# A hybrid DiT step with product-key experts: key numbers summed on Pool, and another passage from gates to experts

## What is computed

```python
def peer(h, wq, keys, u, v):
    q = (x @ wq).reshape(t, PEER_HEADS, 2, PEER_HALF)
    sc = jnp.einsum('thpc,hpnc->thpn', q, keys)
    s_top, i_top = lax.top_k(sc, PEER_TOPK)
    cand = (s_top[:, :, 0, :, None] + s_top[:, :, 1, None, :]).reshape(t, PEER_HEADS, -1)
    cs, ci = lax.top_k(cand, PEER_TOPK)
    i1 = jnp.take_along_axis(i_top[:, :, 0], ci // PEER_TOPK, axis=-1)
    i2 = jnp.take_along_axis(i_top[:, :, 1], ci % PEER_TOPK, axis=-1)
    idx = i1 * PEER_N_KEYS + i2
    g = jax.nn.softmax(cs, axis=-1)
    a = jnp.einsum('thkd,td->thk', u[idx], x)
    act = jax.nn.gelu(a, approximate=False) * g
    return jnp.einsum('thk,thkd->td', act, v[idx])
```

## Time and profile before

| | |
|---|---|
| three runs | 3451.32, 3452.62, 3455.44 us; median 3452.62 |
| the profiled execution | 3446.14 us, its span 3444.0 us |
| busy in the span | PE 91%, DVE 85%, Pool 54%, ACT 31% |
| mean granted PE clock | 0.958 |
| layer 0: routing, gates, experts | 461 to 655, 655 to 784, 784 to 1867 |
| layer 1: routing, gates, experts | 1980 to 2198, 2198 to 2327, 2327 to 3410 |

### The profile page before, as it was taken

How to read it: one execution, slowest core, us unless ns; L and a number is a source line. 1 busy time by engine, 2 the same in 40 slices (tenths; PEclk the granted TensorE clock), 3 DMA queues, 4 the chain that set the end, 5 groups by cost and what they waited for, 6 DMA issues and landing times.

```text
span 3444.0 us, 50075 instructions
## 1 busy us (share of the span) xinstructions
PE 3141.0 (91%) x15686; PEld 2593.3 (75%) x15686; DVE 2929.7 (85%) x5454; ACT 1053.0 (31%) x1587; POOL 1860.0 (54%) x1415
## 2 busy tenths in 40 slices
PE   7898999398999999999998795398999999999997
PEld 4455555277999999999997463377899999999996
DVE  2654189897999999999998599887999999999998
ACT  2132111143333333333333210243333333333332
POOL 0000023485677877776673033585777777766663
PEclk9999999699999999999999897699999999999999
DMA  4131253148999999999996010149999999999995
GB/s 203 49 122 53 92 213 135 49 213 349 408 410 409 402 403 383 410 407 410 398 407 256 25 49 0 73 195 376 397 410 409 408 402 396 406 409 400 408 401 206
DMA packets 244489, 994.43 MB, mean 289 GB/s; under 512 B 22592, under 2 KB 72512, under 8 KB 204864
## 3 DMA queue, kind: packets, MB, share of 16 engines
q0 software_dynamic: 147456, 536.94, 39.5%
q1 hardware_dynamic: 96960, 456.52, 33.3%
HBM read 940.15 MB, written 53.22 MB: 288 GB/s over the span
## 4 chain that ended last, share of the span: by engine, by line
PE 78%; DVE 13%; issue 4%; DMA 3%; POOL 1%; ACT 1%; DVEq 0%; POOLq 0%; SPq 0%; ACTq 0%
PE bankA L1143 10%; PE bankA L1145 10%; PE bankA L1144 10%; PE bankD L1131 6%; PE bankD L1156 6%; PE bankD L1157 6%; PE bankD L1155 6%; PE bankA L1235 5%; PE bankA L1157 3%; PE bankA L1156 3%; PE bankA L1155 3%; PE bankD L1281 2%; DMA rows<-in_u,idxc 2%; PE bankA L1227 1%; DVE topi L873 1%
## 5 line engine op out<-in xcount | busy, mean ns | idle before, releaser
L514 POOL DMA_INDIRECT rows<-in_u,idxc x512 | 736.8, 1439 | 238.1 <-issue 132.8
L514 POOL DMA_INDIRECT rows<-in_v,idxc x512 | 661.1, 1291 | 267.5 <-issue 128.2
L1143 PE MATMUL bankA<-hh,uh 128*128 128x384 f32 x2048 | 690.0, 337 | 23.6 <-ACT htok L584 13.8
L1145 PE MATMUL bankA<-hh,ul 128*128 128x384 f32 x2048 | 689.6, 337 | 0.0
L1144 PE MATMUL bankA<-hl,uh 128*128 128x384 f32 x2048 | 688.2, 336 | 0.0
L1005 DVE SCALAR_TENSOR_TENSOR acc<-rows,a,acc 128x1024 f32<-128x1024 f32 x512 | 634.3, 1278 | 6.7 <-DMA rows<-in_v,idxc 5.5
L996 DVE CUSTOM_DVE_ANT_0 rows<-rows,htok 128x1024 f32<-128x1024 f32 x512 | 607.2, 1218 | 25.3 <-DMA rows<-in_u,idxc 22.8
L476 POOL TENSOR_TENSOR mask<-mask,topf 128x1280 f32<-128x1280 f32 x32 | 91.8, 2891 | 818.7 <-DVE mask L924 818.7
L568 ACT ACTIVATE wt<-bankA 128x384 f32<-128x384 f32 x256 | 125.9, 492 | 1064.8 <-PE bankA L1145 848.7
L1143 PEld LDWEIGHTS bankA<-hh,uh 128*128 128x128 f32 x2048 | 386.4, 189 | 36.3 <-ACT htok L584 14.4
L1156 PE MATMUL bankD<-vl,wh 128*128 128x512 f32 x1024 | 399.8, 390 | 0.0
(11 more groups left out here) (181 smaller groups left out, 4484.0 us busy)
## 6 DMA issues: line engine op xcount, KB each, us to landing
uraw<-in_uT SPq DMA_DIRECT2D x128, 1024.0 KB
vraw<-in_vP SPq DMA_DIRECT2D x128, 1024.0 KB
gates_scratch<-gbuf SPq DMA_DIRECT2D x12, 4096.0 KB, 11.6
gp<-gates_scratch SPq DMA_DIRECT2D x64, 768.0 KB
sq<-in_ada SPq DMA_DIRECT2D x14, 2048.0 KB, 7.9
wch<-in_ada SPq DMA_DIRECT2D x10, 2048.0 KB, 7.9
wch<-in_wq SPq DMA_DIRECT2D x8, 2048.0 KB, 8.0
rows<-in_u,idxc POOLq DMA_INDIRECT x512
```

The costliest lines, as they stand in the source:

```text
L514: pool.indirect_dma_start(out=rows[:, j, :], out_offset=None, in_=table.rearrange("l e d -> (l e) d"), in_offset=bass.IndirectOffsetOnAxis ...
L1143: pe.matmul(abank[c], hi, hh[:, k, :], start=k == 0, stop=False)
L1145: last = pe.matmul(abank[c], lo, hh[:, k, :], start=False, stop=k == K - 1)
```

## The change

- Pool makes the key numbers alone (`pick_keys`): one fold of both masks from 16 columns to 8, then to 4, to 2, and two adds that write i12. DVE's `key_numbers` is gone; DVE waits for mask_scaled before it writes topf, and for mask_done before it writes mask. All eight heads' i12 are waited for by mask_done after the softmax.
- hl is computed by Pool, between heads 6 and 7. hh is cast by ACT as soon as the scores are copied, before the Exp, and the transposes to htok come before the gates.
- Each gate stage of Pool is followed by three gathers (the third by two). The first five row buffers lie in hT, which nobody reads any more by then.
- The last block of gates is stored in two parts: key numbers 0 to 7 first (256 KB), then, behind the load of v pair 1, the rest (3840 KB). dense_begun comes when the last gate is copied, without waiting for a store; v pair 0 is loaded at once, gates 0 to 3 after the small store, gates 4 to 7 after the rest has landed. acc is cleared between the rows of u and those of v.
- Buffers lie elsewhere in SBUF.

```diff
         with ExitStack() as dn:
-            hh = sb("hh", [P, K, TD], F32R, where=dn)
-            hl = sb("hl", [P, K, TD], F32R, where=dn)
+            htok = sb("htok", [P, GT, D], where=dn)
             uraw = sb("uraw", [P, 2, 2 * D], where=dn)
+            rowsB = sb("rowsB", [P, RING - TILES, D], where=dn)
             uh = sb("uh", [P, 2, D], F32R, where=dn)
             ul = sb("ul", [P, 2, D], F32R, where=dn)
             vraw = sb("vraw", [P, 2, 2 * D], where=dn)
...
+            gp1 = sb("gp1", [P, TD // TB, 4, TB], where=dn)
+            acc = sb("acc", [P, GT, D], where=dn)
+            gap = sb("gap", [P, 5440], where=dn)
+            hh = sb("hh", [P, K, TD], F32R, where=dn)
+            hl = sb("hl", [P, K, TD], F32R, where=dn)
             wl = sb("wl", [P, 2, TD], F32R, where=dn)
-            gp = sb("gp", [P, 2, TD // TB, 4, TB], where=dn)
-            rows = sb("rows", [P, RING, D], where=dn)
-            htok = sb("htok", [P, GT, D], where=dn)
-            acc = sb("acc", [P, GT, D], where=dn)
+        gp = (gp0, gp1)
+        hrows = hT[:, :, :].rearrange("p k t -> p (k t)").rearrange("p (r d) -> p r d", d=D)
+        row_buf = [hrows[:, j, :] if j < TILES else rowsB[:, j - TILES, :] for j in range(RING)]
+        htok_bank = [bankA[0], bankD[1]]
...
@@ -362,7 +370,15 @@
                 for b in range(TD // TB):
                     n = L * (TD // TB) + b
                     sp.wait_ge(g_out, (n + 1) * (TB // HOT) + 2)
-                    sp.dma_start(gates_d[b], gbuf[:, b % 2, :, :]).then_inc(stored[b % 2], 16)
+                    if b < TD // TB - 1:
+                        sp.dma_start(gates_d[b], gbuf[:, b % 2, :, :]).then_inc(stored[b % 2], 16)
+                    else:
+                        sp.dma_start(gates_d[b][:, 0:GROUP, :], gbuf[:, b % 2, 0:GROUP, :]).then_inc(edge_stored, 16)
+
+            def store_rest(L):
+
+                b = TD // TB - 1
+                sp.dma_start(gates_d[b][:, GROUP:NKEY, :], gbuf[:, b % 2, GROUP:NKEY, :]).then_inc(stored[b % 2], 16)
...
             def expert_loads(L):
 
-                def group(g, last=False):
+                def group(g, first=False, last=False):
                     for p in range(GROUP // 2):
                         q = g * GROUP + (2 * p + L * NKEY)
                         if not (last and p >= 2):
                             sp.wait_ge(ul_ready, q + (2 + 2))
                             load_u(L, g * (GROUP // 2) + (p + 2), p % 2)
+                            if first and p == 0:
+                                sp.wait_ge(stored[1], 16 * ((L + 1) * DT + 1))
+                                load_gates(4, 1)
                             sp.wait_ge(vl_ready, q + (2 + 2))
                             load_v(L, g * (GROUP // 2) + (p + 2), p % 2)
                         if p % 2 and not last:
@@ -392,11 +411,13 @@
                             load_gates(g * GROUP + (2 * p + 6), p // 2)
 
                 sp.wait_ge(dense_begun, L + 1)
+                load_v(L, 0, 0)
+                sp.wait_ge(edge_stored, 16 * (L + 1))
                 load_gates(0, 0)
-                load_v(L, 0, 0)
                 load_v(L, 1, 1)
-                load_gates(4, 1)
-                with sp.Fori(0, GROUPS - 1) as g:
+                store_rest(L)
+                group(0, first=True)
+                with sp.Fori(1, GROUPS - 1) as g:
                     group(g)
                 group(GROUPS - 1, last=True)
...
                     if L == 0:
                         load_later(8, len(ADA_LATER))
                     sp.wait_ge(routed, L + 1)
+                    sp.wait_ge(mask_done, PH * (L + 1))
                     load_u(L, 0, 0)
                     load_u(L, 1, 1)
                     store_gates(L)
...
-                with pool.Fori(0, PH) as h:
+                def pick_keys(h):
...
                     last.then_inc(mask_scaled, 1)
                     pool.wait_ge(mask_scaled, h + (L * PH + 1))
                     pool.sem_inc(pool_passed, 1)
+                    m3 = mask[:, :, :, :, :].rearrange("p c t k a -> p (c t k) a")
+                    pool.tensor_tensor(m3[:, :, 0:8], m3[:, :, 0:8], m3[:, :, 8:16], ALU.add).then_inc(mask_folded, 1)
+                    pool.wait_ge(mask_folded, h * 2 + (L * PH * 2 + 1))
+                    pool.sem_inc(pool_passed, 1)
+                    pool.tensor_tensor(m3[:, :, 0:4], m3[:, :, 0:4], m3[:, :, 4:8], ALU.add).then_inc(mask_folded, 1)
+                    pool.wait_ge(mask_folded, h * 2 + (L * PH * 2 + 2))
+                    pool.sem_inc(pool_passed, 1)
+                    pool.tensor_tensor(m3[:, :, 0:2], m3[:, :, 0:2], m3[:, :, 2:4], ALU.add).then_inc(mask_halved, 1)
+                    pool.wait_ge(mask_halved, h + (L * PH + 1))
+                    pool.sem_inc(pool_passed, 1)
                     for c in range(2):
-                        last = pool.tensor_tensor(mask[:, c, :, :, 0:TOPK // 2], mask[:, c, :, :, 0:TOPK // 2],
-                                                  mask[:, c, :, :, TOPK // 2:TOPK], ALU.add)
+                        last = pool.tensor_tensor(i12[:, :, c, slice(h * TOPK, (h + 1) * TOPK) if isinstance(h, int) else bass.ds(h * TOPK, TOPK)],
+                                                  mask[:, c, :, :, 0], mask[:, c, :, :, 1], ALU.add)
                     last.then_inc(mask_done, 1)
 
-                with pool.Fori(1, DT + 1) as i:
+                def gather(table, slot, g):
+
+                    pool.indirect_dma_start(
+                        out=row_buf[slot], out_offset=None, in_=table.rearrange("l e d -> (l e) d"),
+                        in_offset=bass.IndirectOffsetOnAxis(ap=idxc[:, g % 2, slot:slot + 1], axis=0),
+                    ).then_inc(row_ready[slot], 16)
...
+                with pool.Fori(0, PH - 1) as h:
+                    pick_keys(h)
+                pool.wait_ge(split_h, L + 1)
+                pool.tensor_tensor(hl[:, :, :], hT[:, :, 0:TD], hh[:, :, :].bitcast(F32), ALU.subtract
+                                   ).then_inc(h_split, 1)
+                pick_keys(PH - 1)
+                pool.wait_ge(idx_ready, L + 1)
+                pool.wait_ge(h_split, L + 1)
+                pool.wait_ge(htok_full, (L + 1) * GT)
+                pool.tensor_copy(idxc[:, 0, :], idx[:, 0:RING]).then_inc(idx_copied, 1)
+                pool.wait_ge(idx_copied, L * 2 * ITERS * (ROWS // RING) + 1)
+                pool.wait_ge(rows_free, L * 2 * ITERS * ROWS + RING)
+
+                for i in range(1, DT + 1):
...
@@ -496,25 +561,16 @@
                                 hot[:, b, 0, :, :], hot[:, b, 0, :, :],
                                 pickT[:, 2, bass.ds(t0, HOT)].unsqueeze(2).to_broadcast([P, HOT, P]),
                                 ALU.mult).then_inc(hotg_ready, 1)
-                pool.wait_ge(idx_ready, L + 1)
-                pool.wait_ge(dense_begun, L + 1)
-                for stage, table in enumerate((u_d, v_d)):
...
+                    for j in range(3 * i - 3, min(3 * i, RING)):
+                        gather(u_d, j, 0)
+                for g in range(1, ROWS // RING):
+                    gather_ring(u_d, 0, L * 2 * ITERS, g)
+                with pool.Fori(1, ITERS) as i:
+                    for g in range(ROWS // RING):
+                        gather_ring(u_d, i, i + L * 2 * ITERS, g)
+                with pool.Fori(0, ITERS) as i:
+                    for g in range(ROWS // RING):
...
             def route_copies(L):
 
+                act.copy(hh[:, :, :], hT[:, :, 0:TD]).then_inc(split_h, 1)
+                for j in range(GT):
+                    act.wait_ge(htok_full, L * GT + j + 1)
+                    act.copy(htok[:, j, :], htok_bank[j][:, :]).then_inc(htok_ready, 1)
                 act.wait_ge(gexp_in, L + 1)
                 act.activation(gt[:, :, :], gt[:, :, :], ACT.Exp).then_inc(gexp_out, 1)
 
-                act.copy(hh[:, :, :], hT[:, :, 0:TD]).then_inc(split_h, 1)
...
-                def key_numbers(h):
-
-                    v.wait_ge(mask_done, h + (L * PH + 1))
-                    v.sem_inc(dve_passed, 1)
-                    for c in range(2):
-                        last = v.tensor_reduce(i12[:, :, c, bass.ds(h * TOPK, TOPK) if not isinstance(h, int)
-                                                   else slice(h * TOPK, (h + 1) * TOPK)],
-                                               mask[:, c, :, :, 0:TOPK // 2], AX.X, ALU.add)
-                    return last
...
+                    then_h(last)
                     if not first:
-                        last = key_numbers(h - 1)
-                    then_h(last)
+                        v.wait_ge(mask_scaled, h + L * PH)
+                        v.sem_inc(dve_passed, 1)
                     v.tensor_copy(topf[:, 1, :, :], topi[:, 1, :, :])
...
+                    if not first:
+                        v.wait_ge(mask_done, h + L * PH)
+                        v.sem_inc(dve_passed, 1)
...
```

(28 more changed lines are left out.)

50 lines of the change are left out of this document (23 added, 27 removed).

## The result

| | before | changed |
|---|---|---|
| median, us (lowest to highest, 4 runs each) | 3452.95 (3451.32 to 3455.44) | 3415.68 (3411.62 to 3420.68) |
| ratio, 95% interval | | 0.9903 [0.9887, 0.9918] |
| profiled execution, us; span | 3446.14; 3444.0 | 3415.33; 3413.5 |

Beside the last experiment the changed kernel ran again on another chip: 3417.51 us against 3446.38, ratio 0.9911 [0.9898, 0.9925]. The forecast was 3417, and the sum behind it 35.4 us; the two comparisons of medians give 37.3 and 28.9, those of the profiled executions 30.8 and 24.3 (the second by spans, with before's one profile). The ratio on record isn't the quotient of the two medians, which is 0.9892 and lies in its interval; by the ratios the gain is some 33 and 31 us.

What follows compares the result with a forecast made beforehand. Experts fill PE and DMA, so only routing and the passages to and from it could gain. Terms of 14.2 us (layer 0) and 21.2 (layer 1), together 35.4, off the median 3452.62 gave 3417 us, range 3400 to 3434.

Steps and rivals of the forecast that it cites:

- The forecast's last step: From profiled execution to median: 3410.7 us, plus the 6.5 us by which before's median of three runs lay higher, gives 3417.
- Head loop: Routing heads 1 to 7: DVE without mask reductions saves 1.4 us a head; 3.9 us in layer 0, 9.8 in layer 1.
- The block: Between heads 6 and 7: Pool's hl holds DVE's two-operand candidates instruction, losing 6.3 us in each layer.
- Tail: Last mask instruction to first hot: 16.8 us instead of 20.86, so 4.0 us less in each layer.
- Gates: Gate stages: three gathers issued between stages nearly vanish in Pool's idle time, costing 0.4 us, at worst 2.5.
- Start of the experts: After the last gate: earlier start gains at most 16.5 and 17.6 us, less 3.5 for the store's rest: 13.0 and 14.1.
- The debt isn't paid back quickly: Experts after the start: each needs 403 of DMA's 409 GB/s, so DMA work left over is repaid only slowly.
- The bound named as the least: Start of the experts: DMA starts 12.8 us sooner but has a net 1.04 MB more to move, leaving 10.3 us.
- Rival 2: Start of the experts: the store's rest holds gathers, rows come late, 10 us or less gained a layer; 3425 or 3431; chance 0.17.
- term 5: The forecast's term for the start of the experts: 13.0 us gained in layer 0 and 14.1 in layer 1.
- Rival 1: Between heads 6 and 7: Pool's hl blocks nobody, giving 3401 us; chance 0.17.
- the slower one: Pool's folds: time goes by short runs, 5.8 us a fold over 160 runs, total over 3530 us; chance 0.03.

Runs made afterwards that it cites:

- the last experiment, experiment 12: Changed kernel with Pool's hl in two instructions, an eighth between heads 6 and 7, the rest after DVE's last topf; 3408.28 us, ratio 0.9883 against before.
- experiment 1: Changed kernel with only hl moved back from Pool to DVE, behind idx; 3413.60 us, ratio 0.9905 against before.
- experiment 2: Changed kernel with hl still on Pool but started only once DVE has finished topf of the last head; 3413.89 us, ratio 0.9901 against before.
- the six profiles: Same program from first hot on: changed kernel twice, hl on DVE, hl later, key numbers on DVE, hl in two; mean hot to gelu 40 467.6 and 466.4 us.
- experiment 9: Changed kernel with the rest of the last gate store split into pieces, most placed ahead of later expert groups; 3415.39 us, ratio 0.99 against before.
- Experiments 5 and 8: Changed kernel with all eight gathers after the third gate stage: 3429.28 us, ratio 0.9941; changed kernel with the store's rest written twice: 3439.35 us, ratio 0.997.

## Why the prediction came out as it did

The total was right to 1.3 us, but with luck. By stages the terms of the sum gave 29.7 us where 35.4 were put: the start of the experts, gates included, fell 7 short, layer 0's heads held, the tails gave 1.9 more and layer 1's heads 1.1 less. Then 4.6 more were lost in stages at which nothing was put. The profiled executions are 30.8 and 24.3 us apart, less than forecast. The forecast's last step added the 6.5 us by which before's profiled execution lay under its median; the changed kernel's first profiled execution lay 0.35 under its own, and that difference closed most of the gap. What makes it was not found, and on the second chip the medians are only 28.9 apart.

- **Bound.** Only routing and passages could gain: so it was. The stretch of experts in the earlier trace rows holds the same busy PE and DMA as before (1094.51 of 1130 us and 0.90).
- **Head loop.** In layer 0 the wait for the scores was right: heads 2 to 6 last 25.4 us, as two units of PE do, and the stage came out at -2.2 against -2.4 (without the block, 3.5 us against 3.9). In layer 1 a head saves 25.67 - 24.53 = 1.14 us, not 1.4: the two new waits of DVE cost more than was put. The gap ahead of L942 (wait on mask_scaled) is 0.34 us, where 0.15 + 0.05 were put, and the one ahead of L970 (wait on mask_done) is 0.26 where before had 0.15, for which nothing was put. That makes 8.0 us in seven heads instead of 9.8.
- **The block.** Taken at 6.3 from one row on the other direction; 5.8 in layer 0 and 5.7 in layer 1, shown by experiment 1, where hl is gone from Pool, and by 2 and 12, where it has moved. The sign named for it was DVE idle some 6 us before its candidates; the profile instead shows the four instructions themselves as lasting 6.41. By the Trainium skill (SBUF — State Buffer, Who interferes with whom) a two-input DVE instruction and a GpSimd instruction that reads SBUF lock each other out for a whole instruction: the trace agrees, 6.41 for 0.69 us. The same section says that copies and casts on DVE can lock too in their two-port modes; the cast of 1.78 for 0.20 us in experiment 2 and the copy of 2.81 for 0.19 in the tail agree, though no run shows the mode in which they ran. The prediction counted neither.
- **Tail.** 5.0 and 4.9 instead of 4.0. Pool's chain there was put at 14.0 and took 13.0: softmax's two-operand instructions mostly waited for Pool and not Pool for them (folds of 3.22 and 1.88 for 2.86 and 1.52).
- **Gates.** -0.4 a layer was put; from the first hot to the last store are 123.08 us in layer 0 and 123.58 in layer 1, 123.33 and 123.21 before: +0.25 and -0.37. Three gathers vanish in Pool's idle time.
- **Start of the experts.** This is the mis-sized term. 13.0 and 14.1 less the 0.4 of the gates were put; at gelu 40 the six profiles give 8.8 and 10.8, the first profile 10.9 and 11.3. Up to gelu 5, to which layer 0 was costed, the term was right: 12.6 put, 9.3 to 14.1 measured, 12.1 in the mean. "PE goes on without a gap" nearly held too, with 0.7 to 3.2 us of idle PE before the first spread in layer 0 and at most 1.5 in layer 1.

  The step that failed is "The debt isn't paid back quickly", by which nothing was put behind gelu 5. From there to gelu 10 the first profile takes 44.7 us where before took 41.5, with the waits for rows shown above, and from gelu 10 to 40 both take the same; the mean loss of the six is 3.3 in layer 0, and in layer 1 12.9 us are won by gelu 5 and 10.8 left at gelu 13, where 13.7 were put. With the rest in pieces (experiment 9) the loss isn't there. The bound named as the least, 10.3 from DMA's bytes, was therefore the nearest.

  Experiments 5 and 8 price this stretch by bytes: 3.15 MB moved into it cost 6.4 us, 2.0 a MB, and 3.93 MB added cost 5.9 and 10.7 by stages and 10 to 12 by the ratios, 1.5 to 2.9 a MB; 409 GB/s are 2.4. The 3.5 us taken off for the 3.9 MB were too few. Rival 2 (10 or less of term 5, through late rows) thus described the mechanism better than the forecast did, and layer 0's size; the tail gave part of the difference back.
- **Not foreseen.** The passage between the layers takes 142.4 to 148.9 us in the thirteen profiles behind the change, whose program is the same there, and 143.5 in before. The granted clock over it is 0.88 in before (1859.5 to 2003.0) and 0.86 in experiment 2 (1845.9 to 1994.8), whose passage is the longest; but experiment 1 has 0.90 and 146.5 us, so the mean clock alone doesn't order them. What sets the length was not found; whether the change makes the passage longer or before had a short one stays open. The 6.5 us between before's profile and its median stay open as well.

Rival 1 (hl blocks nobody) is refuted; so is the slower one: Pool's folds over 160 short runs take 2.86 us, by elements.

## What to carry to other kernels

An engine that has time isn't free to take any instruction: look at what the other engine does in that very window, and put a long Pool instruction where DVE only searches (MAX8, FIND_INDEX8, MATCH_REPLACE8), not where it adds, copies or casts. Where a stretch is full on DMA, cost what enters and leaves it in bytes over the measured rate, and expect an earlier start to bring little more than that once the bytes have caught up. And before explaining 3 us by stages, profile the same program twice.

## What the runs showed of the hardware

- One Pool instruction holds DVE's add of two SBUF tiles (6.41 us for 0.69) and its copy or cast from one (1.78 for 0.20), and leaves MAX8, FIND_INDEX8 and MATCH_REPLACE8 at their 0.74, 0.22 and 0.21 us.
- A Pool subtraction of 128x3072 took 6.65 us, one of 128x384 0.99 and one of 128x2688 5.85; DVE needs 3.35 for the first.
- Behind 4.56 us of idle PE the granted clock was 0.50 for some 3 us, and the first nine matmuls of 128x384 took 0.52 to 0.66 us and not 0.33; behind 24 short transposes they took 0.33 to 0.34 from the second on.
- In a stretch with DMA at 404 to 408 GB/s, bytes moved into it or added cost 1.5 to 2.9 us a MB (experiments 5 and 8).
- Profiles whose program is the same from the first hot on differ by up to 4.2 us until gelu 40 of layer 0 and by up to 2.5 from there to gelu 127, while the routing stages repeat to 0.1 us.
